# A two-layer diffusion trunk on one core: gathered rows gated and added by GpSimd, first low halves moved, low halves in two operations

## The reference, cut to what matters

```python
h = rmsnorm(x, norm_mix_l) * (1.0 + sc1) + sh1
y, new = mixer_sublayer(h, lp_mix, ctx, lam_init)
x = x + g1 * y
h = rmsnorm(x, norm_ffn_l) * (1.0 + sc2) + sh2
x = x + g2 * hier_moe(h, *lp_moe)
```

## Time and profile before

| | |
|---|---|
| three runs | 1731.72, 1726.76, 1733.15 us, median 1731.72 |
| the profiled execution | 1727.18 us, of which the span is 1725.2 us |
| TensorE busy | 1667.7 us, 97% of the span, 9997 matmuls |
| VectorE busy | 1045.9 us, 61% |
| ScalarE busy | 872.9 us, 51% |
| GpSimd busy | 661.8 us, 38% |
| mean granted TensorE clock | 0.997 of full speed |
| layer 0's experts, layer 1's experts | about 640 to 858 us, 1488 to 1706 us |

### The profile page before, as it was taken

The page is one execution under the profiler, slowest core; times in us unless marked ns, Lnnn a source line. Parts: engine busy times, 40 slices in busy tenths (PEclk is TensorE's granted clock), DMA queues, the critical chain, the costliest instruction groups (busy, mean ns, idle before and its releaser), DMA issues.

```text
span 1725.2 us, 30932 instructions
## 1 busy us (share of the span) xinstructions
PE 1667.7 (97%) x9997; PEld 1329.3 (77%) x9997; DVE 1045.9 (61%) x1868; ACT 872.9 (51%) x1499; POOL 661.8 (38%) x426
## 2 busy tenths in 40 slices
PE   6999999999999999999989999999999999999997
PEld 5788787677888877777767888777778887777775
DVE  3127577564461189999850374775635413899997
ACT  2443344444443357788644334454445334587874
POOL 0645563334467621011125555533344765201102
PEclk9999999999999999999999999999999999999999
DMA  8723343343555559999865234334354553999994
GB/s 335 269 90 103 105 147 125 102 178 136 186 196 217 184 192 408 372 370 366 304 224 196 98 104 138 108 121 146 123 184 160 208 200 142 336 385 370 372 365 157
DMA packets 120847, 367.46 MB, mean 213 GB/s; under 512 B 11964, under 2 KB 34044, under 8 KB 120704
## 3 DMA queue, kind: packets, MB, share of 16 engines
q1 hardware_dynamic: 95024, 323.99, 51.9%
q0 software_dynamic: 6624, 24.18, 3.6%
q10 hardware_dynamic: 19056, 17.52, 3.3%
HBM read 341.71 MB, written 23.93 MB: 212 GB/s over the span
## 4 chain that ended last, share of the span: by engine, by line
PE 52%; issue 17%; DVE 14%; POOL 8%; ACT 4%; DMA 3%; SPq 1%; ACTq 0%; DVEq 0%; POOLq 0%
PE G L1340 13%; PE G L1342 12%; PE G L1341 11%; POOL wlo L810 6%; DVE wlo L1860 4%; ACT whi L982 2%; PE O L1397 2%; PE T L1652 2%; PE S L1638 1%; DMA x_scratch<-pA 1%; DVE pA L1860 1%; PE O L1682 1%; PE S L1340 1%; DVE pB L1860 1%; PE S L1342 1%
## 5 line engine op out<-in xcount | busy, mean ns | idle before, releaser
L810 POOL TENSOR_TENSOR wlo<-raw,whi 128x1024 fp32r<-128x1024 f32 x198 | 483.0, 2445 | 571.3 <-ACT whi L974 571.2
L1340 PE MATMUL G<-whi,hhi 128*128 128x512 f32 (+1 forms) x1440 | 578.5, 402 | 12.3 <-DVE wlo L1860 6.4
L1342 PE MATMUL G<-whi,hlo 128*128 128x512 f32 (+1 forms) x1440 | 557.7, 387 | 0.0
L1341 PE MATMUL G<-wlo,hhi 128*128 128x512 f32 (+1 forms) x1440 | 557.1, 387 | 0.0
L1340 PEld LDWEIGHTS G<-whi,hhi 128*128 128x128 f32 x1440 | 270.4, 188 | 90.7 <-DVE wlo L1860 16.5
L1342 PEld LDWEIGHTS G<-whi,hlo 128*128 128x128 f32 x1440 | 270.5, 188 | 57.5
L1341 PEld LDWEIGHTS G<-wlo,hhi 128*128 128x128 f32 x1440 | 271.1, 188 | 46.9
L974 ACT ACTIVATE whi<-raw 128x1024 fp32r<-128x1024 f32 x204 | 214.6, 1054 | 106.9 <-PE G L1342 71.2
L1860 DVE TENSOR_TENSOR wlo<-raw,whi 128x1024 fp32r<-128x1024 f32 x150 | 179.8, 1220 | 6.3 <-ACT whi L982 3.3
L982 ACT ACTIVATE whi<-raw 128x1024 fp32r<-128x1024 f32 x144 | 152.6, 1060 | 32.5 <-PE G L1342 18.5
L1183 ACT ACTIVATE prob<-prob,am 128x384 f32<-128x384 f32 x64 | 38.9, 609 | 117.0 <-DVE am L2151 58.7
(11 more groups left out here) (384 smaller groups left out, 2411.0 us busy)
## 6 DMA issues: line engine op xcount, KB each, us to landing
raw<-in_units SPq DMA_DIRECT2D x426, 512.0 KB, 5.1
pA<-in_units SPq DMA_DIRECT2D x78, 512.0 KB, 5.9
pB<-in_units SPq DMA_DIRECT2D x72, 512.0 KB, 6.3
h_sorted<-sig POOLq DMA_DIRECT2D x12, 514.0 KB, 7.1
hs<-h_sorted POOLq DMA_DIRECT2D x10, 514.0 KB, 7.4
y_sorted<-yo POOLq DMA_DIRECT2D x10, 512.0 KB, 7.1
bias<-in_nat_bias ACTq DMA_DIRECT2D x16, 256.0 KB, 3.2
kT<-in_units SPq DMA_DIRECT2D x6, 512.0 KB, 4.8
```

The source lines that it names most:

```text
L810: lo_done.of(nc.gpsimd.tensor_tensor(wlo[:, k, :], raw[:, POS_OF[g] % RAW, :], whi[:, k, :].bitcast(F32), ALU.subtract))
L1340: nc.tensor.matmul(dst, st_hi, mv_hi, start=start, stop=False)
L1341: nc.tensor.matmul(dst, st_hi, mv_lo, start=False, stop=False)
L1342: return nc.tensor.matmul(dst, st_lo, mv_hi, start=False, stop=stop)
```

## The change

- The first three low halves of each layer move from VectorE to GpSimd, and every low half that GpSimd makes becomes two operations of 512 columns.
- Tile 0 of the first norm is scaled by ScalarE, between the squares of tiles 1 and 2; ScalarE's high halves of units 0 to 2 move by a few places.
- The tables of the first expert tile come three units later.
- GpSimd multiplies the gathered rows of tiles 1 and 2 by the gate and adds them to `x`; VectorE does so for tile 0. TensorE's four products with the identity go, and VectorE waits for TensorE's half banks one by one. The buffer `yo` is released by TensorE and no longer by GpSimd.

```diff
+EARLY = TILES * 7
@@ gpsimd
                 def split(g):
                     pool.wait_ge(*hi_done.at(l, g))
                     k = g % CONV
-                    lo_done.of(nc.gpsimd.tensor_tensor(wlo[:, k, :], raw[:, POS_OF[g] % RAW, :], whi[:, k, :].bitcast(F32),
-                                                       ALU.subtract))
+                    for half in (slice(0, 512), slice(512, 1024)):
+                        ins = nc.gpsimd.tensor_tensor(wlo[:, k, half], raw[:, POS_OF[g] % RAW, half],
+                                                      whi[:, k, half].bitcast(F32), ALU.subtract)
+                    lo_done.of(ins)
...
-                        if s[0] == "gemm" and g + 2 == CONV:
-                            pool.wait_ge(*lo_done.at(l, CONV - 1))
+                        if s[0] == "gemm" and g == 0:
+                            for n in range(CONV):
+                                split(n)
...
-                        need(last_pe, TILES - 1)
-                        yo_free.of(nc.gpsimd.tensor_tensor(dummy[:, 12:13], ones[:, 0:1], ones[:, 0:1], ALU.mult))
+                        need(g_in, 3)
+                        for t in range(1, TILES):
+                            need(y_in[t], 0)
+                            own(nc.gpsimd.tensor_tensor(yacc[:, t, :], yacc[:, t, :], gbc[:, t // 2, :], ALU.mult))
+                            ev_pool.of(nc.gpsimd.tensor_tensor(x[:, t, :], x[:, t, :], yacc[:, t, :], ALU.add))
@@ scalar
+                            if w == 0 and t == 2:
+                                scaled(0)
                             sq_act.of(nc.scalar.activation(junk, x[:, t, :], ACT.Square, accum_out=st[:, t:t + 1]))
-                        if w == 0:
-                            split(0)
...
-                        act.wait_ge(*rstd_pool.at(l, TILES * w + 1))
-                        xn_act.of(nc.scalar.activation(xn[:, 1, :], x[:, 1, :], ACT.Copy, scale=st[:, 1:2]))
+                        scaled(1)
+                        if w == 0:
+                            split(0)
...
+                            if w == 0 and c == 1:
+                                split(1)
                             if w == 0 and c == 3:
-                                split(1)
+                                split(2)
                                 late_rows(0)
                             if w == 0 and c == 5:
-                                split(2)
@@ tensor
-                        need(last_act, 0)
-                        need(y_in[1], 0)
-                        nc.tensor.matmul(last_bank(1, 0), ident[:, :], yacc[:, 1, 0:512], start=True, stop=False)
                         need(last_act, 1)
...
+                        for t in range(TILES):
+                            for hf in range(2):
+                                if (t, hf) == (0, 1):
+                                    pe.wait_ge(*yo_act.in_tile(l, NT - 1, 1, 0))
+                                last_pe.of(back_to_tokens(t, hf, start=True, stop=True))
+                        yo_free.of(keep_busy(S[:, 0, 0:P], BUSY_END))
@@ vector
-                        for t in (0, 2):
+                        for t in (0, 2) if w else (2,):
...
                                 low(0)
-                                first_low(0)
                                 low(1)
...
-                                if n == LAST_SEL and first:
+                                if n == LAST_SEL + 3 and first:
                                     tables()
...
                             if t:
-                                own(*(tt(yacc[:, t, h], last_bank(t, hf), gbc[:, t // 2, h], ALU.mult)
-                                      for hf, h in enumerate(halves)))
+                                need(ev_pool, EARLY + t - 1)
                             else:
-                                own(*(tt(yacc[:, t, h], yacc[:, t, h], last_bank(t, hf), ALU.add)
-                                      for hf, h in enumerate(halves)))
+                                dve.wait_ge(*y_in[t].at(l, 0))
                                 own(tt(yacc[:, t, :], yacc[:, t, :], gbc[:, t // 2, :], ALU.mult))
+                                own(tt(x[:, t, :], x[:, t, :], yacc[:, t, :], ALU.add))
+                            for hf in range(2):
+                                h = slice(hf * 512, (hf + 1) * 512)
+                                need(last_pe, 2 * t + hf)
+                                ins = tt(yacc[:, t, h], last_bank(t, hf), gbc[:, t // 2, h], ALU.mult)
```

More of the change, by code:

```diff
@@ L1005, in _, with scaled @@
                         w = s[1]
+                        def scaled(t):
+                            act.wait_ge(*rstd_pool.at(l, TILES * w + t))
+                            xn_act.of(nc.scalar.activation(xn[:, t, :], x[:, t, :], ACT.Copy, scale=st[:, t:t + 1]))
                         if w:
@@ L1377, in keep_busy @@
                     for _ in range(n):
-                        nc.tensor.matmul(where, ident[:, :], ident[:, :], start=True, stop=True)
+                        mm = nc.tensor.matmul(where, ident[:, :], ident[:, :], start=True, stop=True)
+                    return mm
                 pe.wait_ge(*yo_act.in_tile(l, 0, 1, -1))
@@ L1456, in _ @@
                             keep_busy(S[:, 0, 0:P], BUSY_BEGIN)
-                        need(xn_dve, 2 * w + 1)
-                        need(xn_act, w)
+                        need(xn_dve, 2 * w)
+                        need(xn_act, w + 1)
                         for c in range(KD if w else 4):
@@ L1797, in back_to_tokens @@
                                                     **flags)
-                        need(last_act, 0)
-                        need(y_in[1], 0)
-                        nc.tensor.matmul(last_bank(1, 0), ident[:, :], yacc[:, 1, 0:512], start=True, stop=False)
                         need(last_act, 1)
-                        back_to_tokens(0, 0, start=True, stop=True)
-                        pe.wait_ge(*yo_act.in_tile(l, NT - 1, 1, 0))
-                        last_pe.of(back_to_tokens(0, 1, start=True, stop=True))
-                        nc.tensor.matmul(last_bank(1, 1), ident[:, :], yacc[:, 1, 512:D], start=True, stop=False)
-                        back_to_tokens(1, 0, start=False, stop=True)
-                        last_pe.of(back_to_tokens(1, 1, start=False, stop=True))
-                        need(y_in[2], 0)
-                        for hf in range(2):
-                            nc.tensor.matmul(last_bank(2, hf), ident[:, :], yacc[:, 2, hf * 512:(hf + 1) * 512],
-                                             start=True, stop=False)
-                            mm = back_to_tokens(2, hf, start=False, stop=True)
-                        last_pe.of(mm)
-                        keep_busy(S[:, 0, 0:P], BUSY_END)
+                        for t in range(TILES):
[4 more added lines that the diff above has]
+                        yo_free.of(keep_busy(S[:, 0, 0:P], BUSY_END))
         @block.vector
@@ L1929, in low @@
                                 hl_dve.of(tt(hlo[:, c, :], chunk(c), hhi[:, c, :].bitcast(F32), ALU.subtract))
-                        def first_low(g):
-                            need(hi_done, g)
-                            lo_done.of(tt(wlo[:, g % CONV, :], raw[:, POS_OF[g] % RAW, :], whi[:, g % CONV, :].bitcast(F32),
-                                          ALU.subtract))
                         if w:
                             unit_low(0, 0)
-                        for t in (0, 2):
+                        for t in (0, 2) if w else (2,):
                             dve.wait_ge(*rstd_pool.at(l, TILES * w + t))
@@ L1974, in _ @@
                                 low(3)
-                                first_low(1)
                             elif c > 3 and c % 2:
@@ L1978, in _ @@
                                 low(c)
-                                if c < KD - 1:
-                                    first_low(c // 2)
                         if w:
@@ L2264, in _ @@
                         for t in range(TILES):
-                            halves = [slice(hf * 512, (hf + 1) * 512) for hf in range(2)]
-                            dve.wait_ge(*y_in[t].at(l, 0))
-                            need(last_pe, t)
                             if t:
-                                own(*(tt(yacc[:, t, h], last_bank(t, hf), gbc[:, t // 2, h], ALU.mult)
-                                      for hf, h in enumerate(halves)))
-                            else:
-                                own(*(tt(yacc[:, t, h], yacc[:, t, h], last_bank(t, hf), ALU.add)
-                                      for hf, h in enumerate(halves)))
+                                need(ev_pool, EARLY + t - 1)
+                            else:
+                                dve.wait_ge(*y_in[t].at(l, 0))
                                 own(tt(yacc[:, t, :], yacc[:, t, :], gbc[:, t // 2, :], ALU.mult))
```

(5 more changed lines are left out.)

## The result

Over 20 runs of each, the changed kernel takes 1731.99 us (1729.45 to 1736.51) and the kernel before 1728.24 us (1726.21 to 1733.15): a ratio of 1.0019, interval 1.0012 to 1.0026. So it is slower, by 3.75 us, and well inside the half per cent that the forecast called the same. The forecast's sum was +3.85, and its time 1735.5: 3.5 too high, because the sum was put on 1731.72, the median of three runs, and the median of twenty is 1728.24. That the sum agrees to 0.1 us is luck: several of its steps were wrong, and the errors cancelled.

A forecast was written before the change was run, and what follows sets the result against it. TensorE, busy 97% of the span, was taken as the bound, so only its work or waits count; terms summed to +3.85 us, put on the median 1731.72 for a forecast of 1735.5, range 1718 to 1745.

The forecast's parts named there:

- point 3: Layer 1's norm: tiles 0 and 1 rooted by the last add, transposes 3.0 us after it instead of 4.2: -1.2.
- point 4: First projection without VectorE's unit 0 low half: -1.15 in layer 0; in layer 1, -1.8 together with the norm.
- point 1: Last tile, both layers: VectorE's low halves take turns with four GpSimd operations, so TensorE ends late: +8.0 us per layer.
- point 5: Low halves in two: -1.15 at each of two attention waits per layer, -4.6; waits for GpSimd +0.6.
- 2, the end of a layer: Layer's end without TensorE's four identity products: last add 9.6 us after the units' end instead of 11.7, -2.1 per layer.
- rival C: Last-tile collision as forecast, but the attention keeps its waits as second halves take the port first: 1740.5 us; chance 0.12.
- Rival B: Halves work against TensorE: four low halves a layer 1 us late, attention gain halved: 1746 us; chance 0.15.
- 6, the tables: First expert tile's table operations, three units later, shorten TensorE's wait for the hidden rows' split: -0.5 per layer, -1.0.

The follow-up runs named there:

- kernel 6: Kernel 1 with GpSimd's low halves whole again, one operation of 1024 columns each: 1727.07 us, 0.9985.
- kernel 7: Kernel 1 with the tables of the first expert tile back at unit 8 instead of unit 11: 1722.04 us, 0.9957.
- kernel 1: The changed kernel with the last tile and the layer's end taken back to the kernel before: 1722.44 us, 0.9955.
- kernel 2: The kernel before with only the change's last tile and layer's end: 1741.68 us, 1.0067.
- kernel 12: Kernel 8 plus four unread GpSimd operations in the last tile, both inputs full rows in SBUF: one run, span 1731.6 us against 1715.1.
- kernel 8: Kernel 1 with VectorE gating and adding tile 0 early, TensorE adding tiles 1 and 2, and ScalarE scaling tile 0 early: 1718.0 us, 0.9937.
- Kernel 5: The changed kernel with ScalarE scaling tile 0 before its wait for the last add, and `yo` released earlier: 1731.53 us, 1.001.
- kernels 4: The changed kernel with each of GpSimd's four last-tile operations split into two of 512 columns: 1726.6 us, 0.9976.
- 10: Kernel 8 with GpSimd's low halves in four operations of 256 columns instead of two of 512: 1719.4 us, 0.994.
- kernel 9: Kernel 8 with ScalarE's first copy of the next modulation rows ahead of unit 2's high half: 1717.59 us, 0.9924.
- kernel 3: The changed kernel with GpSimd's four gating and adding operations started only after VectorE's last low half: 1724.8 us, 0.9971.

## Why the sum came out, and which steps failed

Four steps of the forecast failed. The norm of layer 1 (point 3) was to gain 1.2 us and gained 0.1, because ScalarE's scaling of tile 0 stood on the path. The start of layer 0 (point 4) was to gain 1.15 and gained nothing: the next thing to be late was a load. The turn (point 1) was priced at a whole GpSimd operation, 2.37, and measured 2.16, so that the last tile cost 7.0 a layer and not 8.0. Of the two attention waits (point 5) the second did not shorten. The order of the turns, the earlier last add and the size of the halves' gain were right. The sum also left out TensorE's clock.

The markers of the two profiles, after less before: +0.94 at 205 us, -1.27 at 320, -1.88 at the gathers of layer 0, +2.50 at layer 1's first product, +1.80 at 1054, -0.42 at 1167, -1.31 at the gathers of layer 1, +6.96 at the last add. By terms:

| Step | Forecast | Measured |
|---|---|---|
| Layer 0's start (4), with its wait for GpSimd (5) | -0.85 | +0.9; +0.1 in kernels 6 and 7, at full clock |
| Attention, two layers (5) | -4.6 | -4.4 |
| Tables and the experts up to the gathers (6) | -1.0 | -1.5 |
| End of layer 0 with layer 1's start (1 to 4) | +4.1 | +4.4 |
| Layer 1 up to its attention (5) | +0.3 | -0.7 (0.4 of it a shorter wait for the save of `x`) |
| End of layer 1 (1, 2) | +5.9 | +8.3, of it 3.1 the clock |
| Sum | +3.85 | +7.0; without the clock's fall in layer 1 +3.9; with full clock at layer 0's start too about +3.1 |

The +3.9 is no second proof of the forecast: it still holds the clock at layer 0's start, and it compares two single executions.

**1, the turns: right, one term too large.** They are as drawn, to the order of starts; the gather landed after 5.6 us. The mis-sized term is the turn. I put GpSimd's whole 2.37 in front of each low half, a step of 3.57; the step is 3.32, the wait 2.16, and with halves 1.07 where the operation takes 1.27. In both cases it is 0.2 less than GpSimd's operation. That part of it runs beside VectorE's is how I read this; no run tests it. The earlier trace rows had the size: VectorE's 0.68 took 2.88 and 2.76 there, waits of 2.20 and 2.08. Four steps that are 0.25 shorter make 7.0 a layer and not 8. Kernels 1 and 2 show the cost with the gain of the layer's end taken off, 11 to 12 us, and kernel 12 shows the turns alone, 16.5, of which about 2 are the clock by an estimate from its profile: layer 0 is 7.4 longer than in kernel 8, layer 1 some 9. The Trainium skill (SBUF — State Buffer, Who interferes with whom) calls the shared port pair an exclusive lock. The 9.22 us agree that one engine shuts the other out; an exclusive hold for the whole of GpSimd's row would give 2.37 and the rows give 0.2 less.

**2, the end of a layer: right.** The last add ends 9.9 behind the units, where I had 9.6 and before had 11.7.

**3, the norm: failed, and the plainest of the errors.** It said that tiles 0 and 1 are rooted by the last add and that tile 2 alone is late next. The roots were in time. But in ScalarE's order the scaling of tile 0 stands behind the wait for tile 2's last add, and I had placed it beside that wait. It took 1.15 us ahead of the square: the transposes came at 4.1 and not 3.0. Kernel 5 puts the scaling ahead of the wait, and they come at 3.0. With the next step as forecast (3.2 us from the transposes to the first product, against 3.35) points 3 and 4 gave layer 1 0.8 and not 1.8. In the total this was hidden by the turns, which were 1.0 cheaper: an accident.

**4, layer 0's start: failed.** The wait before the first product fell by 1.21, as forecast, and gave nothing. In kernels 4, 6, 7 and 10, where TensorE starts at 29.1 to 29.7 instead of 30.8, it waits 1.5 to 2.0 us at 38 for a copy that ScalarE makes behind unit 2's load, at 36.8 to 37.0, and kernels 6 and 7 reach the wait at 205 us at 205.6, where the kernel before has 205.5. What was late next was a load, on an engine whose order the change had altered too; whether the old order would bring the gain, kernel 9 left open. In the changed kernel's own profile the clock took the gain instead: TensorE's twelve filler products at 25.8 took 2.93 us at 0.50 instead of 1.60, and the first product stands 5.65 behind their start, against 4.12 in kernel 7. There is no wait for the copy then, but at 54.95 TensorE waits 1.17 us, and not 0.53, for ScalarE, which waits for the save of `x`.

**5, the halves: right in sum, wrong in place.** Of two attention waits one went whole (1.76), where I had -1.15; the other stayed, where I had -1.15 as well. The forecast treated both pairs of scalings as one operation that waits once. The second is two operations short enough to meet a half each, which is near to what rival C said of both. The rest is a wait of 0.60 at 251 us that the forecast had not named. Waits for GpSimd fell by 0.6 where I had a rise of 0.6. The halves have little part in it: at 173 us the wait is 0.80 before, 0.57 in kernel 6 with whole low halves and 0.51 with halves in 7. What brought it down I didn't test. Rival B's price, four low halves 1 us late in each layer, is nowhere. (Rival C's sum comes to 1740.8 and not 1740.5; nothing hangs on it.) From the figure of the Trainium skill (GPSIMD Engine Reference, Performance versus the Vector engine), 4497 ns for 2048 columns, I had an estimate of 1.12 for a half, by which halving would be free. Undisturbed pairs take 2.50 to 2.55, so 1.27 a half, and a whole low half 2.40: the fixed part is there.

**6, the tables: not decided.** The stretch before the gathers is 0.6 and 0.9 shorter, but kernel 7, which moves only the tables, shows 0.2 to 0.4 in its trace and nothing clear of noise in its time.

**The clock.** Four profiles have last tiles with waits of that size, two tiles each: the changed kernel, 2, 5 and 12. It fell to the lower level in three of the eight (layer 1 of the changed kernel, both layers of 12), and in no last tile with shorter waits or none. At layer 1's start, between 868 and 887 us, it is at the lower level for 3 to 7 us in the profiles of 1, 2, 3, 4, 7 and 10, and not in the others. Other executions point the same way: three of kernel 2's six took 1736.2 to 1740.0 us at a mean granted clock of 0.994 to 0.996, the other three 1743.4 to 1745.0 at 0.989 to 0.992. So it is likely, though these means don't show where the clock fell, that part of the last tile's price comes and goes from one execution to the next. What decides is open. It wasn't tried to keep TensorE busy there.

## What to carry to other kernels

Price a GpSimd operation by what VectorE has queued at that moment and who waits for it, not by whether GpSimd is idle: each VectorE operation on SBUF that meets it waits for nearly one whole GpSimd operation (2.16 us of 2.37 here), so its size, not the sum of the work, sets the wait. Count VectorE's operations one by one against GpSimd's pieces: halving helped a pair of long ones and did nothing for a pair of short ones. And where a wait is cut, read every engine's order behind the new point, for what stands behind a load or behind a wait for something that comes later.

## What the runs showed of the hardware

- With both engines' operations queued they took turns, one each. A VectorE low half of 1024 columns then waited 2.16 us for a GpSimd operation of 2.37, 1.07 for one of 1.27, and 1.67 for one of 1024 columns with a single full input; GpSimd's own operations stretched from 2.37 to 3.24 us. A pair of VectorE scalings with one full input, 0.48 us alone, took 2.35 beside two halves.
- VectorE's operations with a PSUM input weren't held in the rows read: the split of the hidden rows at 858.22 takes 0.41 us, its length without company, beside GpSimd's operation of 857.29 to 860.53. In kernel 3 two half multiplies from PSUM at 858.98 take 1.29 us, as they do alone, beside one of 857.94 to 861.16.
- The granted clock can differ where the code is the same: from 24 to 28 us it is 0.50 in kernel 1 and 1.00 in kernel 7, which differ only in the tables at 640 us. Twelve filler products take 2.92 us in the one and 1.60 in the other.
